# A load placed between the two halves of the input, and the second half's transposes placed behind the first eight matmuls

## The reference

```python
hn = rms_norm(h, mix_norm_pre[layer])                  # h is x, 256 x 1024
b_gate, c_gate, h = jnp.split(hn @ w_in, 3, axis=-1)   # w_in is 1024 x 3072
```

## Time and profile before

| | |
|---|---|
| median of 3 runs | 1110.22 us (1109.82 to 1112.21) |
| the profiled execution | 1111.5 us, span 1109.4 us |
| TensorE busy | 1100.3 us, 99% of the span |
| VectorE, ScalarE, GpSimd busy | 755.9, 593.4, 54.5 us |
| transfers | 193.75 MB, mean 175 GB/s |

### The profile page before, as it was taken

The page is one execution under the profiler, slowest core; times in us unless marked ns, Lnnn a source line. Parts: engine busy times, 40 slices in busy tenths (PEclk is TensorE's granted clock), DMA queues, the critical chain, the costliest instruction groups (busy, mean ns, idle before and its releaser), DMA issues.

```text
span 1109.4 us, 18330 instructions
## 1 busy us (share of the span) xinstructions
PE 1100.3 (99%) x6820; PEld 998.5 (90%) x6820; DVE 755.9 (68%) x1161; ACT 593.4 (53%) x871; POOL 54.5 (5%) x47
## 2 busy tenths in 40 slices
PE   7999999999999999999999999999999999999998
PEld 7998888888999999999988888888999989999987
DVE  6976655564697677676667565655787787989970
ACT  6436654453654655454567454645446756666640
POOL 0100000000000000000000000000110011122210
PEclk9999999999999999999999999999999999999999
DMA  9655756666495454542247657572635564655770
GB/s 279 187 174 169 244 163 204 231 214 203 128 269 152 135 160 124 150 133 76 95 122 221 197 173 238 201 245 71 191 96 181 171 210 134 189 175 184 231 244 19
DMA packets 215670, 193.75 MB, mean 175 GB/s; under 512 B 9609, under 2 KB 190909, under 8 KB 215613
## 3 DMA queue, kind: packets, MB, share of 16 engines
q1 hardware_dynamic: 215401, 192.88, 56.1%
q10 hardware_dynamic: 212, 0.09, 0.0%
HBM read 191.88 MB, written 1.05 MB: 174 GB/s over the span
## 4 chain that ended last, share of the span: by engine, by line
PE 98%; DVE 1%; DMA 1%; ACT 0%; SPq 0%; issue 0%; ACTq 0%
PE ps L665 14%; PE ps L667 14%; PE ps L666 14%; PE ps L610 8%; PE ps L611 8%; PE ps L612 8%; PE ps L764 6%; PE ps L766 6%; PE ps L765 6%; PE ps L819 2%; PE ps L845 2%; PE ps L834 1%; PE ps L853 1%; PE ps L679 1%; PE ps L713 1%; PE ps L677 1%
## 5 line engine op out<-in xcount | busy, mean ns | idle before, releaser
L1648 DVE TENSOR_TENSOR w_lo<-raw,w_hi 128x1024 fp32r<-128x1024 f32 (+1 forms) x298 | 398.9, 1383 | 59.6 <-ACT w_hi L1209 59.2
L1209 ACT ACTIVATE w_hi<-raw 128x1024 fp32r<-128x1024 f32 (+1 forms) x298 | 331.5, 1158 | 121.9 <-PE ps L667 31.6
L610 PE MATMUL ps<-x_hi,w_hi 128*128 128x256 f32 x656 | 186.7, 285 | 0.0
L612 PE MATMUL ps<-x_hi,w_lo 128*128 128x256 f32 x656 | 185.6, 283 | 0.0
L611 PE MATMUL ps<-x_lo,w_hi 128*128 128x256 f32 x656 | 185.6, 283 | 0.0
L665 PE MATMUL ps<-w_hi,x_hi 128*128 128x512 f32 (+1 forms) x328 | 129.4, 394 | 0.0
L667 PE MATMUL ps<-w_hi,x_lo 128*128 128x512 f32 (+1 forms) x328 | 127.5, 389 | 0.0
L666 PE MATMUL ps<-w_lo,x_hi 128*128 128x512 f32 (+1 forms) x328 | 127.3, 388 | 0.0
L610 PEld LDWEIGHTS ps<-x_hi,w_hi 128*128 128x128 f32 x656 | 125.8, 192 | 1.3 <-issue 1.3
L611 PEld LDWEIGHTS ps<-x_lo,w_hi 128*128 128x128 f32 x656 | 125.9, 192 | 0.0
L612 PEld LDWEIGHTS ps<-x_hi,w_lo 128*128 128x128 f32 x656 | 125.8, 192 | 0.0
(11 more groups left out here) (231 smaller groups left out, 1780.0 us busy)
## 6 DMA issues: line engine op xcount, KB each, us to landing
raw<-in_ffn_w_gate_up SPq DMA_DIRECT2D x176, 256.0 KB, 4.1
raw<-in_w_up SPq DMA_DIRECT2D x44, 512.0 KB, 4.4
raw<-in_ffn_w_down SPq DMA_DIRECT2D x24, 768.0 KB, 6.3
raw<-in_conv_w_in SPq DMA_DIRECT2D x24, 512.0 KB, 5.4
raw<-in_w_q SPq DMA_DIRECT2D x48, 256.0 KB, 4.4
raw<-in_w_kv SPq DMA_DIRECT2D x48, 256.0 KB, 4.1
raw_v<-in_w_kv SPq DMA_DIRECT2D x48, 256.0 KB, 4.2
raw<-in_w_in SPq DMA_DIRECT2D x20, 512.0 KB, 4.5
```

The costliest lines, as they stand in the source:

```text
L610: nc.tensor.matmul(o, wh[:, k0 + k, c], hi[:, k, :], start=(k == 0), stop=False)
L612: ins = nc.tensor.matmul(o, wl[:, k0 + k, c], hi[:, k, :], start=False, stop=(k == kt - 1))
L1209: nc.scalar.activation(w_hi[:, s, a * ph.cols:b * ph.cols], src, ACT.Copy)\
L1648: nc.vector.tensor_tensor(w_lo[:, s, c], src, w_hi[:, s, c], ALU.subtract)\
```

## The change

On SP, `load` gets an argument for the halves that it loads. The first half of chunk 0 is now loaded behind the first half of x, and the second half of chunk 0 behind the second half of x. On TensorE the transposes stand in a function `turn_input(half)`. Half 0 runs where all of them ran; half 1 runs inside `feature_major_first`, behind the first 8 matmuls. ScalarE, VectorE and GpSimd keep their programs.

```diff
-            def load(ph, j, i):
+            def load(ph, j, i, parts=(0, 1)):
...
-                for part in range(2):
+                for part in parts:
...
                 for t in range(2):
                     sp.dma_start(h[:, t, c], a["x"][0, t * P:(t + 1) * P, c]).then_inc(landed_in, 16)
-            load(phases[0], 0, 0)
+                load(phases[0], 0, 0, parts=(half,))
             load(phases[0], 1, 0)
...
-            def feature_major_first(ph, j, hi, lo, bi):
+            def feature_major_first(ph, j, hi, lo, bi, second_half):
...
                             nc.tensor.matmul(o, wh[:, k, c], hi[:, k, :], start=(k == 0 and m == 0), stop=False,
                                              skip_group_check=True)
+                    if part == 0:
+                        second_half()
                     for k in range(k0, k1):
                         pe.wait_ge(norm_split, norm_count(bi, 0, 0, k))
...
+            def turn_input(half):
+
+                pe.wait_ge(x_rest_in if half else x_in, 2 * 16)
+                for k in range(4 * half, 4 * half + 4):
+                    for t in range(2):
+                        c = (k % 2 * 2 + t) * P
+                        ins = nc.tensor.transpose(ps[:, 4 + k // 2, c:c + P], h[:, t, k * P:(k + 1) * P], ident[:])
+                    if k % 2 == 1:
+                        ins.then_inc(turned_in, 1)
+                    if k == 1:
+                        pe.wait_ge(gain_in, len(VECS[0]) * 16)
+                        turn_vectors(0, 3).then_inc(turned_in, 1)
+
             pe.wait_ge(ident_in, 16)
-            for k in range(KD):
-                if k % 4 == 0:
-                    pe.wait_ge(x_in if k == 0 else x_rest_in, 2 * 16)
-                for t in range(2):
...
+            turn_input(0)
...
-                            feature_major_first(ph, 0, x_hi, x_lo, 0)
+                            feature_major_first(ph, 0, x_hi, x_lo, 0, second_half=lambda: turn_input(1))
```

More of the change, by code:

```diff
@@ L776, in turn_vectors @@
                 return nc.tensor.transpose(ps[:, bank, c:c + n], vec_rows[0:n, g, :], ident[0:n, 0:n])
-            pe.wait_ge(ident_in, 16)
-            for k in range(KD):
-                if k % 4 == 0:
-                    pe.wait_ge(x_in if k == 0 else x_rest_in, 2 * 16)
-                for t in range(2):
[L783 to L789, removed]
+            def turn_input(half):
[9 more added lines that the diff above has]
+                        turn_vectors(0, 3).then_inc(turned_in, 1)
+            pe.wait_ge(ident_in, 16)
+            turn_input(0)
             def turn_probs(src, at_, n):
```

## The result

| | before | changed |
|---|---|---|
| median of 22 runs | 1111.34 us (1109.73 to 1112.37) | 1112.53 us (1112.28 to 1113.21) |
| profiled execution | 1111.5 us, span 1109.4 | 1112.55 us, span 1110.5 |

The ratio is 1.0015, with a 95% interval of 1.0009 to 1.0021; it follows the means of the runs (1112.58 and 1110.97), while the medians alone give 1.0011. The change is 1.2 us slower in the median: clear of noise, and by the best estimate under the 0.2% that the prediction set as its bound. The three runs shown ahead of the prediction had a median of 1110.22; over 22 runs the kernel before is at 1111.34.

A forecast was written before the change was run, and what follows sets the result against it. TensorE was taken as the bound, 98% of the chain, with 0.92 us idle to win. The earlier load, the transposes' cost and the chain to w_lo summed to +0.9 on 1110.22: 1111.1 us, range 1109.5 to 1113.2.

The forecast's parts named there:

- The load (1): Start: weight half lands at about 6.7, ScalarE's split starts 0.65 earlier, first matmul at 9.06 instead of 9.71.
- The transposes (2): Behind the first eight matmuls: eight transposes cost 1.71, TensorE 1.06 late, of which 0.6 us remain at chunk 1.
- The chain (3): ScalarE's x_hi 4 to 7, then w_hi and VectorE's w_lo end late; chunk 1 at about 18.3, sum +0.9 us.
- What was costed at nothing (4): The norm's diag and chunk 2's second half come later but in time, with cover of 1.2 and 1.3 us.
- The slow pace for longer: Rival: transposes amid chunk 0's matmuls put off the pace's rise; +1.9, at worst +3.8; chance 0.26, 0.13 beyond 2.2.
- The rival with nearly free transposes: Pace rises sooner, the eight transposes cost 0.7, the chain ends near 17.6: +0.2, so 1110.4; chance 0.12.
- Chunk 2 was not late: Rival: chunk 2's second half loads in 6.6 or more, TensorE waits; up to 1 us; chance 0.08 with late weights.
- the weights were not late: Rival: weight half not landed at 7.96, gain of 0.65 lost, TensorE about 1.2 later: 1111.5; chance 0.08 with chunk 2 late.

The follow-up runs named there:

- e2_turn_only: The changed kernel with the loads in their old order, so only the transposes move: 1113.23 us, ratio 1.0017 to the kernel before.
- look_before_1: The kernel before, unchanged, executed once more for a profile; first weight half split at 9.64, slow start: 1113.03 us.
- e3_reorder: The changed kernel with the second half of chunk 0 split before x_hi and x_lo 4 to 7 are made: 1112.27 us, ratio 1.0005 to the kernel before.
- look_before_3: The kernel before, unchanged, executed again for a profile; first product at 10.23, fast from its start: 1110.54 us.
- look_before_4: The kernel before, unchanged, executed again for a profile; first product at 9.41, fast from its start: 1109.79 us.
- e8_after_filled: The changed kernel with four float32 matmuls of constants behind the first eight transposes, filling TensorE's idle time: 1111.70 us, ratio 1.0002 to the kernel before.
- e7_quarter_early: The kernel before with the first weight half loaded and split in two pieces, and eight matmuls of constants ahead of the first transpose: 1110.09 us, ratio 0.9986.
- e6_before_early: The kernel before with eight float32 matmuls of constants ahead of the first transpose, while TensorE waits for x: 1111.18 us, ratio 0.9998.

## Why the prediction was right, point by point

**The load (1).** ScalarE's split started without a wait, at 8.09 for a forecast 7.96, and the first product at 9.20 (9.06); x itself came 0.25 later in this execution (first transpose at 4.94). The landing was wrong: the prediction had the weight half at 6.7, from the place in the order. The transfers in the changed kernel that were issued at 1.66 and at about 2.7, us to landing:

```profile
raw<-in_conv_w_in SPq DMA_DIRECT2D x1, 512.0 KB, 6.2
...
h<-in_x SPq DMA_DIRECT2D x1, 256.0 KB, 6.6
```

The weights landed at 7.86, with 0.2 us to spare and not 1.2. The half of x behind them needed 6.6 and was there at about 9.3, forecast 8.6. So the place in the order gave a lower bound here, not the landing. That the split still had no wait was in part luck: `e2_turn_only` and look_before_1 show the same kind of transfer coming 0.6 and 1.0 later than in the trace of before.

**The transposes (2).** 11.08 to 12.64 is 1.56 us, forecast 1.71; TensorE was 1.06 late behind them, forecast 1.06. This figure agrees because two errors of 0.15 cancel: the product gained 0.51 instead of 0.65, and the transposes cost less. The pace rose at 12.9 and not at 14.0. TensorE's own path ended at 17.83, forecast 18.0.

**The chain (3).** x_hi at 12.17 (forecast 12.03), the split at 13.75 (13.6), w_lo done at 18.34 (18.2), chunk 1 at 18.39 (18.3), behind a wait of 0.40 (0.1 to 0.5). For the pair of profiled executions the forecast sum was +0.9, measured +1.05 in time and +1.1 in span. By my estimate 0.25 of both is x, which came later in the changed execution (4.94 against 4.69), so the agreement to 0.15 is closer than one pair of traces can vouch for. `e3_reorder` showed that the wait is this chain's. The cover of 0.4 that the prediction saw ahead of the second half of chunk 0 was all but gone: TensorE was there at 14.80, not 15.1, and went on at 14.86.

**What was costed at nothing (4).** diag was done at 19.86 (20.0) and used at 21.36 in the trace; chunk 2's w_lo were done at 22.5, forecast 23.5, since the load of its second half took 3.5 and not 5.3. The cover of chunk 2 was larger than feared.

**The rivals.** The slow pace for longer did not come: the rise came directly behind the transposes. Its ground, that transposes don't help to raise the clock, is refuted by look_before_3 and look_before_4, where TensorE had done nothing else before its fast products. The rival with nearly free transposes did not come for the changed kernel as it is; in the trace of `e8_after_filled`, with the idle time filled, they cost 0.8 for eight. Chunk 2 was not late; the weights were not late. The price of late weights, +1.2, counted TensorE's own path only and left out the chain of (3), which starts with the first product too: `e2_turn_only` has just that case, and its median is 1.6 above the kernel before.

**What the prediction had wrong** is the base of its sum. It took one moment of the rise, that of the profiled execution, for both kernels, and set +0.9 on a median of three runs of which two belonged to the group below 1110.4. The kernel before has two kinds of start: of its 22 runs, ten lie at 1110.45 or below and twelve at 1111.22 or above. Against the median of the upper group (1111.68) the change loses 0.85, which is the forecast +0.9, and against that of the lower one (1110.08) 2.5. None of its 22 runs is near the lower group. So the mechanism was right for one kind of start, and the median of the change came out 1.4 above the forecast 1111.1, inside the range because this had been widened by the scatter. (Its upper end is 0.3 too high by its own terms: 1110.22 + 2.2 + 0.5 is 1112.9, not 1113.2.) In the numbers at hand the two groups were to be seen in one place only, the scatter of 2.4 us in three runs, which the prediction named and put down to noise.

## What to carry to other kernels

Work in the shadow of a wait is free only there; moved among products it costs its own time and delays all that is queued behind it on other engines, here by a chain of x_hi, w_hi and three w_lo. When a wait is for a transfer, first cut the transfer and the work behind it to what the first product needs (0.9990 here), before moving work of the waiting engine. And where runs of one kernel fall in groups, take several traces before the edit is costed: the median may rest on a property that the edit removes.

## What the runs showed of the hardware that was not expected

Transposes alone, with 0.55 or 0.88 us of idle time behind them, were enough for a fast pace of the first product in two of five traces of the kernel before; in the other three, with 0.69 to 0.95, they were not. The Trainium skill, page TensorE: Matmul & The Clock Gate, Part 4: PE-mode transpose, says that the full clock doesn't engage for transposes, which don't count as busy in the same way; these traces speak against it. The transposes themselves run at both levels: 0.21 each at the slow pace, 0.10 in `e8_after_filled`.

Short idle times can be enough to lose the pace: after 1.31 us idle in `e7_quarter_early` and 1.65 us in `e6_before_early` the granted clock read 0.50. They need not be: five of the eleven runs of `e6_before_early` show a mean granted clock of 1.000, and are the fastest.

The granted clock shown for the start is not to be trusted: it reads 1.00 while matmuls of 256 columns start 0.21 apart. It read 0.50 only where the pace had been fast before and fell.

The same transfer, issued at 2.60 in the same program, took 5.7 to 7.0 us to land over five traces.
